# The output job of a one-core transformer block: ScalarE empties the turned rows, and three written-out orders change

## The reference, cut to what matters

```python
h = rmsnorm(x, norm_mix_g)                       # x: 2048 x 1024, float32
proj = h @ w_in                                  # q, k, v, pool and memory queries
merged = sum_i sigmoid(h @ w_gate_i + b_gate_i) * (y_i @ w_branch_i)   # 3 branches
x = x + merged @ w_out
hm = rmsnorm(x, norm_mlp_g)
x = x + square(relu(hm @ w_up)) @ w_down         # 4096 wide
out = rmsnorm(x, norm_final_g)
```

## Time and profile before

| what | us |
|---|---|
| median of 3 runs (lowest to highest) | 2606.76 (2605.96 to 2606.80) |
| profiled execution, own time | 2605.82 |
| its span, first to last instruction | 2604.0 |
| mean granted TensorE clock | 0.998 |

### The profile page before, as it was taken

How to read it: one execution, slowest core, us unless ns; L and a number is a source line. 1 busy time by engine, 2 the same in 40 slices (tenths; PEclk the granted TensorE clock), 3 DMA queues, 4 the chain that set the end, 5 groups by cost and what they waited for, 6 DMA issues and landing times.

```text
span 2604.0 us, 33036 instructions
## 1 busy us (share of the span) xinstructions
PE 2567.9 (99%) x12065; PEld 2127.3 (82%) x12065; DVE 1724.0 (66%) x2390; ACT 1157.0 (44%) x2129; POOL 557.3 (21%) x510
## 2 busy tenths in 40 slices
PE   8999999999999999999999999999999999999998
PEld 6888888888887887888887888888888888888886
DVE  8676657666466655658778666765557576575886
ACT  6344535344334433424455455654545243342433
POOL 1444200000022152336554542000000111111100
PEclk9999999999999999999999999999999999999999
DMA  5677555676446787777797665633355585767653
GB/s 180 214 254 260 184 182 178 186 223 223 140 130 242 242 254 251 229 270 258 236 301 248 217 223 168 224 110 117 108 172 159 110 221 115 183 150 163 196 178 114
DMA packets 346764, 508.71 MB, mean 195 GB/s; under 512 B 33208, under 2 KB 213484, under 8 KB 346604
## 3 DMA queue, kind: packets, MB, share of 16 engines
q1 hardware_dynamic: 318956, 431.08, 51.0%
q0 software_dynamic: 27648, 75.51, 11.6%
HBM read 325.12 MB, written 181.40 MB: 195 GB/s over the span
## 4 chain that ended last, share of the span: by engine, by line
PE 87%; DMA 4%; DVE 3%; POOL 3%; issue 1%; ACT 1%; SPq 0%; POOLq 0%; DVEq 0%; ACTq 0%
PE ps L2315 28%; PE ps L2316 27%; PE ps L2317 27%; DMA t_d<-tin 2%; PE ps L2320 2%; DMA tin<-in_w_down 1%; PE ps L2586 1%; PE ps L2563 1%; PE ps L2486 1%; PE ps L2514 1%; POOL tin L2215 1%; DVE res_lo L1622 0%; POOL tin L2219 0%; DVE s_lo L1616 0%; POOL tin L2217 0%
## 5 line engine op out<-in xcount | busy, mean ns | idle before, releaser
L2315 PE MATMUL ps<-res_hi,s_hi 128*128 128x512 f32 x3084 | 1203.9, 390 | 11.7 <-issue 7.7
L2317 PE MATMUL ps<-res_hi,s_lo 128*128 128x512 f32 x3084 | 1200.8, 389 | 0.0
L2316 PE MATMUL ps<-res_lo,s_hi 128*128 128x512 f32 x3084 | 1200.6, 389 | 0.0
L2315 PEld LDWEIGHTS ps<-res_hi,s_hi 128*128 128x128 f32 x3084 | 579.4, 188 | 135.3 <-issue 11.0
L2317 PEld LDWEIGHTS ps<-res_hi,s_lo 128*128 128x128 f32 x3084 | 579.3, 188 | 120.2
L2316 PEld LDWEIGHTS ps<-res_lo,s_hi 128*128 128x128 f32 x3084 | 579.5, 188 | 118.8
L1111 ACT ACTIVATE s_hi<-piece_f 128x512 fp32r<-128x512 f32 x436 | 274.4, 631 | 486.6 <-PE ps L2317 433.1
L1111 ACT ACTIVATE s_hi<-s_sum 128x512 fp32r<-128x512 f32 x327 | 204.4, 628 | 366.5 <-PE ps L2317 351.1
L1616 DVE TENSOR_TENSOR s_lo<-piece_f,s_hi 128x512 fp32r<-128x512 f32 x432 | 325.2, 753 | 33.0 <-ACT s_hi L1111 25.4
L1616 DVE TENSOR_TENSOR s_lo<-s_sum,s_hi 128x512 fp32r<-128x512 f32 x327 | 243.1, 744 | 104.9 <-ACT s_hi L1111 104.8
L1666 DVE TENSOR_TENSOR u<-u,ps 128x512 f32<-128x512 f32 x109 | 74.7, 686 | 310.8 <-PE ps L2317 310.7
(11 more groups left out here) (187 smaller groups left out, 2498.5 us busy)
## 6 DMA issues: line engine op xcount, KB each, us to landing
proj_d<-c SPq DMA_DIRECT2D x152, 256.0 KB, 3.3
piece_f<-in_w_up SPq DMA_DIRECT2D x32, 1024.0 KB, 7.0
up_d<-c SPq DMA_DIRECT2D x128, 256.0 KB, 2.9
piece_f<-up_d SPq DMA_DIRECT2D x32, 1024.0 KB, 7.1
piece_f<-in_w_gate SPq DMA_DIRECT2D x24, 1024.0 KB, 7.4
w_hi<-parts_d SPq DMA_DIRECT2D x48, 512.0 KB, 3.6
w_lo<-parts_d SPq DMA_DIRECT2D x48, 512.0 KB, 4.9
temp<-proj_d SPq DMA_DIRECT2D x48, 512.0 KB, 6.5
```

The costliest lines, as they stand in the source:

```text
L2315: mm(dst, wh, xh, start=first, stop=False, skip_group_check=joins)
L2316: mm(dst, wh, xl, start=False, stop=False, skip_group_check=joins)
L2317: return mm(dst, wl, xh, start=False, stop=last, skip_group_check=joins)
```

## The change

Four things change, and with the last the end of the program is rewritten.

1. **Output job.** `take_ht` on VectorE no longer serves tiles 38 to 45. ScalarE gets `take_out_rows(n, r)`: eight scaled copies of 128x128 out of the two banks in place of two multiplications of 128x512. Half 1 of tile n-2 stands behind `s_split(n, 6)` and `finish(n-1, C12)`; half 0 of tile n-1 stands ahead of `s_split(n+1, 5)`.
2. **Change from the output job to the up projection** (tiles 45 and 46; operands of job 3).
   - SP: operand 6 is loaded right behind operand 5, and only then the sums of tile 43 are stored (they stood behind operand 4).
   - ScalarE: `r_split(3, 5)` moves from behind `s_split(47, 0)` to ahead of the squares of tile 45.
   - VectorE: `r_low(3, 3)` and `r_low(3, 4)` move from tile 46 into tile 45, and `s_low(46, 4)` behind `r_low(3, 3)`.
3. **Head.** `top_low(p)` is split in its two quarters. The four of quarter 0 come first, and the first product waits for `top_lo >= 5`. `slot_sum(5)`, `head_low(5)` and ScalarE's `r_split(0, 5)` move back; `s_low(1, 0)` to `s_low(1, 4)` come forward.
4. **End.** A new tile `g_out` takes the product of row and gain before the norm is known. The results of tile 109 are added in another split, and the last scaling by the norm is shared by ScalarE and VectorE.

```diff
 SP, jobs, tile n
     if n != OUT_END - 1:
         store_sums(n - 2)
     if last:
         load_slot(j + 1, 4)
-    if n == OUT_END - 1:
-        store_sums(n - 2)
...
     if last:
         load_slot(j + 1, 5)
+    if n == OUT_END - 1:
+        load_slot(j + 1, 6)
+        store_sums(n - 2)
     store_ht(n - 1, 0)
     store_tile(n, 2, C21, 1, 0)
-    if last:
+    if last and n != OUT_END - 1:
         load_slot(j + 1, 6)
 ScalarE, new
+def take_out_rows(n, r):
+    if not out_job(n):
+        return
+    k = across(n)
+    act.wait_ge(xt_rdy, 2 * k + r + 1)
...
+    act.wait_ge(ht_st[r], 16 * k)
+    act.wait_ge(hs_done, 4 * summed(n))
+    if r:
+        act.wait_ge(hs_st, 64 * summed(n))
+    for kk in range(KT):
+        last = op(ht[:, r, kk, :], ps[:, 6 + kk // 4, (kk % 4) * P:(kk % 4 + 1) * P], ACT.Copy,
+                  scale=par[:, PM_MLP + kk:PM_MLP + kk + 1])
+    last.then_inc(ht_done, 1)
 ScalarE, jobs, tile n
     s_split(n, 6)
     if n > lo:
         finish(n - 1, C12, 4)
+    take_out_rows(n - 2, 1)
...
     if first and not (j == OUT_JOB or n > lo and early(j) == 4):
         r_split(j, 4)
     if last:
         r_split(j + 1, 0)
+    if n == OUT_END:
+        r_split(j, 5)
     if has_norm(n - 1):
         row_squares(n - 1)
     if more:
         s_split(n + 1, 0)
     if first:
-        r_split(j, 5)
+        if n != OUT_END:
+            r_split(j, 5)
         r_split(j, 6)
...
+    take_out_rows(n - 1, 0)
     if more:
         s_split(n + 1, 5)
 VectorE, jobs, tile n
-    if first and early(j) < 4:
+    if first and early(j) < 4 and n != OUT_END:
         r_low(j, 3)
...
     take_ht(n - 1, 0)                     # now returns at once for out_job(n)
     if last and early(j + 1) == 1:
         r_low(j + 1, 2)
-    if more:
+    if more and n != OUT_END - 1:
         s_low(n + 1, 4)
     take(n, C12, S4, u2, 3)
+    if n == OUT_END - 1:
+        r_low(j + 1, 3)
+        s_low(n + 1, 4)
     add_row(n, C12, 0, 1)
+    if n == OUT_END - 1:
+        r_low(j + 1, 4)
 VectorE, head_piece
     take_quarters(0)
     take_quarters(1)
-    top_low(0)
+    top_low(0, 0)
     take_quarters(2)
-    top_low(1)
+    top_low(1, 0)
     head_s_low((0, 0))
+    top_low(2, 0)
+    take_quarter(3, 0, 0)
+    top_low(0, 1)
+    top_low(3, 0)
+    take_quarter(3, 0, 1)
     head_s_low((0, 1))
-    top_low(2)
-    take_quarters(3)
-    top_low(3)
+    for p in range(1, 4):
+        top_low(p, 1)
     slot_sum(2)
...
     head_low(1)
-    slot_sum(5)
     s_sums(1, S1)
     s_sums(1, S3)
     s_sums(1, S2)
-    s_low(1, 0)
+    for i in range(3):
+        s_low(1, i)
+    s_sums(1, S4)
     head_low(3)
-    s_low(1, 1)
-    s_low(1, 2)
-    s_sums(1, S4)
+    s_low(1, 3)
+    s_low(1, 4)
+    slot_sum(5)
+    s_low(1, 5)
     head_low(5)
-    for i in range(3, 6):
-        s_low(1, i)
 ScalarE, head_piece: r_split(0, 5) behind s_split(1, 5); the two flags ahead of s_split(1, 3)
 TensorE, head_piece
-    pe.wait_ge(top_lo, 7)
+    pe.wait_ge(top_lo, 5)
 VectorE, last_rows (tile 109; C21 and C12 are no longer made as tiles)
+    row_part(1, 0) += u3
+    row_part(0, 1) += u2
+    with_g(1, 1)                          # g_out = rows * g_fin, 128x512
+    with_g(0, 0)
+    wait for product A22;  row_part(1, 0) += acc(n, A22);  with_g(1, 0);  variance(1, 3)
+    wait for product S4;   row_part(0, 1) += acc(n, S4);   with_g(0, 1);  variance(0, 4)
+    g_out[:, 0, TB:D] *= rrs[:, 0:1]      # with the power of half 0
 ScalarE, last_squares
+    squares of (1, 1), (0, 0), (1, 0);  g_out[:, 1, :] *= rrs[:, 1:2]
+    square of (0, 1);                   g_out[:, 0, 0:TB] *= rrs[:, 0:1]
```

More of the change, by code:

```diff
@@ L299, in build @@
     g_fin = at("g_fin", [P, D], F32, ht_at)
+    g_out = at("g_out", [P, 2, D], F32, job + 128 * KB)
     junk = sb("junk", [P, TB])
@@ L1235, in last_squares, with square @@
                 n, k = NQT - 1, normed(NQT - 1)
-                for done, (i, h) in enumerate(((1, 0), (1, 1), (0, 0), (0, 1))):
-                    act.wait_ge(row_add, 4 * row_quartets(n) + (4 if done == 3 else 3))
+                def square(done, i, h):
+                    act.wait_ge(row_add, 4 * row_quartets(n) + done + 1)
                     act.wait_ge(rs_sum, 4 * k + done)
@@ L1240, in last_squares @@
                         .then_inc(rs_sum, 1)
+                for done, (i, h) in enumerate(((1, 1), (0, 0), (1, 0))):
+                    square(done, i, h)
+                act.wait_ge(rs_pow, k + 1)
+                act.wait_ge(with_gain, 3)
+                op(g_out[:, 1, :], g_out[:, 1, :], ACT.Copy, scale=rrs[:, 1:2]).then_inc(fin_rdy, 1)
+                square(3, 0, 1)
+                act.wait_ge(rs_pow, k + 2)
+                op(g_out[:, 0, 0:TB], g_out[:, 0, 0:TB], ACT.Copy, scale=rrs[:, 0:1]).then_inc(fin_rdy, 1)
             def norm_tiles(n):
@@ L1493, in head_piece @@
                 head_evict(C21)
-                r_split(0, 5)
                 head_evict(C12)
@@ L1567, in take_quarters, with top_low @@
                         take_quarter(p, h, i)
-            def top_low(p):
+            def top_low(p, i):
                 c = slice(p * P, (p + 1) * P)
[L1572 to L1575, removed]
+                lo_, hi_ = ((res_lo[:, 0], res_hi[:, 0]), (b12_lo, b12_hi))[i]
+                dve.wait_ge(top_hi, 2 * p + i + 1)
+                v.tensor_tensor(lo_[:, :, c], x_quarter(0, i)[:, :, c], hi_[:, :, c].bitcast(F32), ALU.subtract)\
+                    .then_inc(top_lo, 1)
             def head_s_low(q):
@@ L1707, in last_rows, with row_part, with_g, variance @@
                 n, k = NQT - 1, normed(NQT - 1)
-                for i in (1, 0):
-                    dve.wait_ge(rs_sum, 4 * k + (2 if i else 4))
+                done = 4 * row_quartets(n)
+                def row_part(i, h):
+                    return rows_of(n)[:, i, h * TB:(h + 1) * TB]
+                def with_g(i, h):
+                    v.tensor_tensor(g_out[:, i, h * TB:(h + 1) * TB], row_part(i, h), g_fin[:, h * TB:(h + 1) * TB], ALU.mult)\
+                        .then_inc(with_gain, 1)
+                def variance(i, sums_):
+                    dve.wait_ge(rs_sum, 4 * k + sums_)
                     v.scalar_tensor_tensor(out=rvar[:, i:i + 1], in0=ss4[:, i, 0:1], scalar=D * EPS, in1=ss4[:, i, 1:2],
                                            op0=ALU.add, op1=ALU.add).then_inc(rs_var, 1)
[L1712 to L1716, removed]
+                dve.wait_ge(ev_dve, POSTS * n + C22)
+                v.tensor_tensor(row_part(1, 0), row_part(1, 0), u3[:], ALU.add)
+                chained(v.tensor_tensor(row_part(0, 1), row_part(0, 1), u2[:], ALU.add))
+                dve.wait_ge(row_add, done + 2)
+                with_g(1, 1)
+                with_g(0, 0)
+                dve.wait_ge(prod, PROD * n + A22 + 1)
+                v.tensor_tensor(row_part(1, 0), row_part(1, 0), acc(n, A22), ALU.add).then_inc(row_add, 1)
+                dve.wait_ge(row_add, done + 3)
+                with_g(1, 0)
+                variance(1, 3)
+                dve.wait_ge(prod, PROD * n + S4 + 1)
+                v.tensor_tensor(row_part(0, 1), row_part(0, 1), acc(n, S4), ALU.add).then_inc(row_add, 1)
+                dve.wait_ge(row_add, done + 4)
+                with_g(0, 1)
+                variance(0, 4)
+                dve.wait_ge(with_gain, 4)
+                dve.wait_ge(rs_pow, k + 2)
+                v.tensor_scalar(g_out[:, 0, TB:D], g_out[:, 0, TB:D], rrs[:, 0:1], None, ALU.mult).then_inc(fin_rdy, 1)
             def take_ht(n, r):
-                if not hosts(n):
+                if not hosts(n) or out_job(n):
                     return
@@ L1799, in jobs @@
                     take_ht(n - 2, 1)
-                    if first and not (j == OUT_JOB or n > lo and early(j) == 4):
+                    if first and not (j == OUT_JOB or n == OUT_END or n > lo and early(j) == 4):
                         r_low(j, 4)
@@ L1842, in jobs @@
                         s_low(n + 1, 3)
+                    if not more and n == NQT - 1:
+                        break
                     take(n, C21, A22, u3, 2)
```

22 lines of the change are left out of this document (11 added, 11 removed).

## The result

The changed kernel takes 2615.45 us (median of six runs, 2611.79 to 2616.56), the kernel before on the same chip 2605.78 (six runs, 2605.21 to 2606.80). The ratio estimated from the runs is 1.0033, with a 95% interval of 1.0023 to 1.0043 (the two medians alone give 1.0037): **slower, by 9.7 us** or 0.3 to 0.4%, beyond the 0.2% that can be told. The forecast was +0.95, a median of 2607.7 in a range of 2602.0 to 2611.9. The profiled execution took 2614.53 us with a span of 2612.7, which is 8.7 more than the span before.

What follows compares the result with a forecast made beforehand. TensorE, busy 99% of the span, was taken to bound the kernel. Head -1.65, end -1.8 and change of jobs +4.4 make +0.95 us: 2606.8 for the profiled execution, 2607.7 as median, range 2602.0 to 2611.9.

Steps and rivals of the forecast that it cites:

- Output job, cost 0: Tiles 38 to 44: ScalarE takes 4.2 us more per tile at no cost; up to 2 us a tile without cover.
- Landing of the stores, 1375.5: Change of jobs: tile 43's sums, stored behind operand 6, land at 1375.5, bounds 1371 and 1379.5.
- Ring order: Change of jobs: descriptors consumed strictly in order put the landing at 1376.5 and the total 1 us longer.
- The signs named in advance: Changed profile: ScalarE idle 5 to 10 us before eight copies, largest mid-span gap at tile 46's A12, transposes near 1395.
- The chain of 21.7 us behind the landing: Change of jobs: ScalarE's list from landing to tile 45's half 1 transposes takes 21.7 us, so they start at 1397.2, costing 4.4.
- rival A: Change of jobs: stores land by 1371 and VectorE bounds instead; total -3.95, 2602.8 us; chance 0.19.
- Clock, 0 in the sum: Change of jobs: the clock falls after an 8 us gap, but TensorE waits for ScalarE anyway, so 0.
- The bound of 1.7: Change of jobs: the most full clock expected to be lost after the gap, 1.7 us.
- the prediction's uncovered case: Change of jobs: if waits for a DMA are paid again at the low clock, uncovered, the total is 1.7 us longer.
- Head, gain 1.65: Head: first product at 26.4, tile 1 at 49.3, its second product 2.0 earlier; gain 1.65 us (0.7 to 2.1).
- End, gain 1.8: End: SP issues the last store at 2597.65 in place of 2599.45; gain 1.8 us (1.0 to 2.2).
- Rival B: Change of jobs: landing at 1380.2 or later, total passes +5.2; priced at 1382.1, +7.5, 2614.3 us; chance 0.10.

Runs made afterwards that it cites:

- head_only: The kernel before with the new head alone: 2605.39 us, -1.0 to the kernel before, ratio 0.9995.
- out_ht: The changed kernel with the old orders of SP, ScalarE and VectorE at the change of jobs; ScalarE's emptying, head and end stay: 2607.22 us, +1.2 to before.
- head_tail: The kernel before with the new head and new end alone: 2603.78 us, -2.4 to before, ratio 0.9990.
- sp_back: The changed kernel with SP's old order at the change of jobs (tile 43's sums stored ahead of loading operands 5 and 6): 2609.18 us, +3.0 to before.
- mix: The changed kernel with SP's old order, ScalarE emptying tiles 38 to 43 only and VectorE tiles 44 and 45: 2605.33 us, -1.0 to before.
- dve_45: sp_back with half 0 of tile 45 emptied by VectorE right behind its C21: 2605.93 us, -0.1 to before.
- dve_45_sp: The changed kernel, SP's new order kept, with half 0 of tile 45 emptied by VectorE: 2610.50 us, +4.1 to before.
- wait_later: The changed kernel with ScalarE's take_out_rows(44, 1) moved behind r_split(3, 5): 2608.80 us, +2.6 to before.
- small_sums: sp_back with GpSimd's four sums of tile 44 on 4 of each 128 columns, the rest left out: 2602.75 us, -3.3 to before.
- pool_late: head_tail with GpSimd in tile 46 summing for S4 first, then waiting for VectorE's C21 before three sums of tile 44: 2607.18 us, +0.8 to before.

## Why the prediction was wrong

- **Output job, cost 0: right.** TensorE is busy 123.00 of 123 us. ScalarE got 80.30 - 59.35 = 20.95 us in six tiles, 3.5 a tile where 4.2 were put.
- **Landing of the stores, 1375.5: right** to 0.4 us (1375.1 on the old scale), and the DMA engines stayed full until then, as argued (share 1.06 and 1.15, at 376 and 354 GB/s):

```profile
1366.00:1370.00 4.00, 3.00 (x14) 2.21 (x13) 4.00 (x3) 0.00 (x0) 0.12 (x1) 1.00 1.06 376
1370.00:1374.00 4.00, 4.00 (x18) 2.93 (x17) 2.27 (x3) 0.00 (x0) 0.00 (x0) 1.00 1.15 354
```

  Ring order as the Trainium skill has it, "DMA: Bandwidth & Descriptors", section "Queues, rings and completion order", stood for 1376.5 where it is taken strictly; the section adds that a later descriptor may finish its write before an earlier one. The measurement is 1.4 us earlier, on the side of the small overtaking that I had read from the rows, but whether the stores did overtake operand 6 no row here shows. The signs named in advance came too: ScalarE idle 8.44 us in front of eight copies, the largest gap in front of A12, no gap in tiles 38 to 44. The transposes near 1395 did not come.
- **The chain of 21.7 us behind the landing: the step that failed.** It took 1400.41 - 1374.14 = 26.3 us. The prediction walked ScalarE's list only, and put "0.9 of waits for VectorE's C21 and semaphores". That is the term that was mis-sized: ScalarE stood 2.18 + 3.03 = 5.2 us in this stretch, both times for VectorE's work. VectorE's list was walked only in rival A, for stores that land early, and from its old times. But VectorE is held as long as ScalarE, since `r_low(3, 4)` needs `r_split(3, 4)`, and its own list from there to C21 is the longer one. The rows of before gave it: `r_low(3, 4)` started at 1375.13 and C21 ended at 1391.47 (1390.79 + 0.68), 16.3 us without idle time, with 3.48, 2.96 and 1.77 us operations in it; two `s_low` of 0.6 join, which stood ahead of `r_low(3, 4)` before its move into tile 45. By that, 1375.5 + 4.0 + 16.3 + 1.2 + 3.5 = 1400.5, and the cost of the part 7.7 us, not 4.4; measured were 8.55. (The prediction's own terms, added again, are 21.8 where it says 22.0; that would have made the chain shorter still.) The earlier trace rows even showed ScalarE idle 3.03 us in front of its C21 **before** the change; a wait that long is no allowance, it says who leads.
- **Clock, 0 in the sum: wrong.** The fall behind the gap of A12 was covered, as argued: TensorE waited for ScalarE again at 1389.01 and 1400.41. But a second fall came in the 3.42 us gap in front of the transposes, where nothing covers it: 2.8 us of clock behind it, and 2.5 us in the end. I had asked only what follows the gap that the change opens, not the gap that closes the chain. The bound of 1.7 was too low because it supposed one stretch of the old length, all of it behind TensorE's start. By the rule of the Trainium skill, "TensorE: Matmul & The Clock Gate", section on HAM oscillation, waits for a DMA between bursts are paid again at the low clock. This trace agrees in the gap of 6.38 us, which goes back to the late stores; the uncovered fall came behind a wait for ScalarE, at 2.8 us where the prediction's uncovered case had 1.7.
- **Head, gain 1.65: right in its gaps, not settled in its size.** The two places where time was to be given back came, 0.52 us at 38.82 and 0.62 at 67.28 (0.5 and 0.4 put). The gaps lost 1.45 us, and 0.95 reached tile 38. The turning of the rows began at 9.14 and took 16.52 us, where it was 8.70 and 16.19, which puts the first product at 27.11 and not at 26.4. But the start of tile 38 scatters over 3 us between traces, and head_only's -1.0 has an interval of over 2 us to each side.
- **End, gain 1.8: 1.4.** The last power took 0.55 us, as put. The last issue ends 4.75 us before the end of the span (2612.7 less 2605.41 + 2.54); before it was 4.21 (2604.0 less 2599.45 + 0.34), and that is the part that was not foreseen.

In sum: head +0.7, chain +4.15, clock +2.5, end +0.4 against the prediction, which makes 7.75 of the 7.76 us by which the profiled execution missed. Rival B came nearest in its total (+7.5, against +8.7 in the profiled execution) by the wrong mechanism, so that is luck: it needed a landing at 1382, and the stores landed at 1375. (By the prediction's own sum the total passes +5.2 at a landing of 1379.75, not 1380.2.)

The runs set the parts thus: 3.6 us for the move to ScalarE with old orders (out_ht less head_tail), 6.7 for the late landing ahead of `r_split(3, 4)` (changed less sp_back), 1.8 between (sp_back less out_ht), within the intervals. Twelve of the sixteen half tiles cost nothing that can be told (mix), and half 0 of tile 45 with its place behind C21 costs 3 to 5.5 us (dve_45, dve_45_sp). That the rest lies with half 1 of tile 44 and its wait is argued from wait_later and from the rows; no run gave that half alone back to VectorE.

## What to carry to other kernels

When a wait holds an engine that feeds another, walk **both** lists from the wait to the point that TensorE needs, with the durations of the rows as they stand, and take the longer; idle time of one of them in the profile of before, ended by the other, hints which that will be (here ScalarE's 3.03 us for VectorE's C21). Work moved off a busy engine to an idle one still costs where the idle one is last in a chain: look at each place where the moved work has someone waiting, not at busy shares. And ask of every gap in the new chain, the last one above all, whether the clock falls behind it and what would cover that.

## What the runs showed of the hardware

- VectorE's `res_lo` of 128x2048 took 2.28 us with GpSimd nearly idle and 2.94 to 3.06 beside GpSimd's additions, its pair of `s_lo` of 128x512 1.31 and 3.49 us; cutting GpSimd's additions short (small_sums) brought the 2.28 and the 1.31 back, but one `res_lo` still took 3.06 us beside a GpSimd addition of 128x16 that took 2.28. GpSimd's additions of 128x512 took 1.28 to 1.29 us with VectorE idle (1405.11 in the changed kernel) and 1.29 to 3.34 beside VectorE.
- The length of a gap alone did not settle whether the granted clock fell. Gaps of 3.41 to 3.43 us in front of the transposes led to it in all five kernels that had them. In the changed kernel the clock fell inside the gap (2.8 us lost behind it), in the other four the loss behind the gap was 1.7 us. One of 3.26 us in pool_late had no fall:

```profile
1395.00:1400.00 5.00, 4.67 (x25) 4.05 (x26) 4.90 (x9) 1.90 (x3) 0.00 (x0) 1.00 0.94 296
```

  A gap of 2.54 us in front of S3 was followed by it in head_only, one of 2.53 in pool_late was not. Even one of 1.85 us in small_sums was followed by it (clock 0.66 from 1375 to 1380), while one of 1.93 in sp_back, at the same product, was not (1.00). What else decides stays open.
